# Second and fourth layer: their first tiles on unnormed, weighted latents, and the two normings' roots taken apart

## The chip, the cores and the metric

The kernel runs on one core of a Trainium2 chip. TensorE (PE) multiplies, VectorE (DVE), ScalarE (ACT) and GpSimd (POOL) work on tiles in SBUF and PSUM, and SyncE (SP) issues the DMAs. The metric is the device time of one execution in microseconds (us), the median of several runs.

## What the kernel computes

Two blocks of two layers each, on 256 latent tokens and 256 context tokens of width 1024. Every layer norms its input, multiplies it by an input matrix, mixes tokens, and then has an MLP of width 4096. Cut to what matters here:

```python
def rms_norm(x, g):
    y = x * lax.rsqrt(jnp.mean(x * x, axis=-1, keepdims=True) + EPS)
    return y * g
def modulate(h, shift, scale):
    return h * (1 + scale) + shift
# first block, layers 0 and 1 (the first and second); second block, layers 2 and 3 (the third and fourth)
a  = modulate(rms_norm(h, norm1_g[l]), sh1, sc1)      # latents
ac = modulate(rms_norm(hc, norm1_g[l]), csh1, csc1)   # context
p, u, vs, q, k, v, gl = split(a @ w_in[l])            # layers 1 and 3 need only k and v of ac
h = h + g2 * sq_relu_mlp(modulate(rms_norm(h, norm2_g[l]), sh2, sc2), w_ff1[l], w_ff2[l])
```

The root belongs to a token, gain and shift to a channel. So (gain*h*root + shift) @ W = root * ((gain*h) @ W) + shift @ W: a tile can be multiplied before the root is known, if its result is scaled by the root and shift @ W is added.

## The kernel before, in words

Everything is held with channels on the partitions: `h` is 8 chunks of 128 channels, each with 256 latent and 256 context columns. A float32 product is made of three matmuls: ACT rounds a tile to `w_h` (lines 1505 to 1513, `round_w`), DVE writes the rest to `w_l` (line 1987, in `split_w`), and inputs are split in the same way into `a_h` and `a_l`. Weights come in tiles of 256 columns (1 MB) through a ring of four slots in SBUF; SP loads a slot again when its tile has been split. Each engine follows its own list of work, written out phase by phase, and waits on semaphores.

The phases around the change are the end of one layer's second MLP product (`to_h` with source `ff`, 16 steps; its last step ends channels 4 to 7) and the entry of the next layer (`norm`, then `b1_in` in the second layer and `s_in` in the fourth). Before the change such an entry goes so:
- DVE adds the last four units to `h` (line 2474). POOL squares and adds the chunks (lines 2756 and 2758), DVE squares the last (line 2485). PE averages over channels with two matmuls (lines 1076 and 1078), for latents and context together, and ACT makes the inverse root (lines 1498 and 1499).
- In the second layer's entry a share of a modulation tile is also summed by DVE between the units (line 2020) and turned by PE (line 984). The PE then transposes a spare tile (line 933, `stay_awake`) 6 times, in the fourth layer's entry 24 times.
- For each of 8 chunks DVE multiplies by gain and root (line 2166, `scaled`), ACT adds the shift and rounds (line 1545, `rounded_norm`), and DVE writes the rest (line 2176, `rest_norm`). First come the latents' 8 chunks. The context's 8 follow: in the second layer among the next tiles (`CTX_CHUNKS`: four chunks, two, two), in the fourth all behind the third tile's split.
- PE takes the first two tiles together, chunk by chunk as they come (`first_tiles`, lines 886 to 891). The fourth layer's third tile needs latents and context (columns 0 to 511), the second layer's third to fifth need latents alone, the sixth both.
- SP loads the new layer's tables (lines 763 to 771, the bias windows at 749) once the last unit has been added to `h`, and only then the ring's next tiles.

The same trick that the change brings to the entry is there already in the MLPs' first tiles: `round_raw`, `rest_raw`, `scale_unit`, `shifted_relu`, `raw_tiles`.

## Time and profile before

| | |
|---|---|
| three runs | 2147.72 us median, 2146.95 to 2152.74 |
| profiled execution | 2148.89 us, span 2147.1 us |
| PE busy | 2097.4 us, 98% of the span |
| DVE busy | 1577.3 us, 73% |
| ACT, POOL busy | 908.8 us, 42%; 461.3 us, 21% |
| entry of the second layer | PE's last MLP matmul at 773.6, first tile at 782.0, third tile at 795.4 |
| entry of the fourth layer | last MLP matmul at 1808.7, first tile at 1814.6, third tile at 1828.4 |

The span is the time from the first to the last instruction that the profiler saw; the execution's own time holds some 1.8 us more around it. PE is busy nearly everywhere, so a change counts by what it does to the few waits of PE, and those lie where one layer hands over to the next.

### The profile page before, as it was taken

How to read it: one execution, taken by the hardware profiler on the slowest of the kernel's cores; microseconds unless marked ns; L12 is line 12 of the kernel's file. 1: busy time of each engine (PE TensorE's matmuls, PEld its weight loads, DVE VectorE, ACT ScalarE, POOL GpSimd, SP SyncE). 2: the span in 40 equal slices, each digit the busy share in tenths (PEclk: the TensorE clock that was granted, in tenths of full speed). 3: DMA queues.
4: the chain of work that ended last, by engine and by line, in shares of the span. 5: the costliest groups of instructions: out<-in, count | busy, mean ns of one | idle time of the engine just before them, and what ended most of it. 6: DMA issues, size and time to landing. Idle time of an engine off the chain costs nothing.

```text
span 2147.1 us, 31174 instructions
## 1 busy us (share of the span) xinstructions
PE 2097.4 (98%) x12421; PEld 1791.0 (83%) x12421; DVE 1577.3 (73%) x2398; ACT 908.8 (42%) x1411; POOL 461.3 (21%) x387
## 2 busy tenths in 40 slices
PE   7999999999999999999999999999999999999998
PEld 4887778888888878899999888778888888759998
DVE  6685667799778886777988777769966664687465
ACT  4313333342333342455444647754233333365454
POOL 0001210322301010212451273322222011204301
PEclk9999999999999999999999999999999999999999
DMA  9642234457675663345766442133766553415552
GB/s 302 227 139 70 67 98 138 157 166 244 239 253 178 215 184 117 117 149 195 237 228 204 138 158 89 50 118 118 235 204 207 190 167 85 99 40 158 177 194 82
DMA packets 247433, 345.36 MB, mean 161 GB/s; under 512 B 31168, under 2 KB 181608, under 8 KB 246520
## 3 DMA queue, kind: packets, MB, share of 16 engines
q1 hardware_dynamic: 245792, 339.11, 48.9%
q10 hardware_dynamic: 1496, 4.24, 0.6%
q8 instruction: 99, 1.62, 0.3%
q14 instruction: 46, 0.38, 0.0%
HBM read 342.23 MB, written 1.10 MB: 160 GB/s over the span
## 4 chain that ended last, share of the span: by engine, by line
PE 84%; DVE 7%; ACT 3%; issue 2%; POOL 2%; DMA 1%; SPq 0%; DVEq 0%; POOLq 0%; ACTq 0%
PE PS L836 24%; PE PS L838 24%; PE PS L837 24%; DVE w_l L1987 2%; PE PS L1129 1%; PE PS L1152 1%; PE PS L1138 1%; POOL h L2743 1%; DMA ring<-in_w_in 1%; PE PS L891 1%; ACT w_h L1512 1%; PE PS L1340 1%; PE PS L886 1%; PE PS L1431 1%; DVE a_l L2176 1%
## 5 line engine op out<-in xcount | busy, mean ns | idle before, releaser
L836 PE MATMUL PS<-a_h,w_h 128*128 128x512 f32 (+1 forms) x2560 | 879.9, 344 | 9.0 <-DVE a_l L2121 4.9
L838 PE MATMUL PS<-a_h,w_l 128*128 128x512 f32 (+1 forms) x2560 | 871.4, 340 | 0.0
L837 PE MATMUL PS<-a_l,w_h 128*128 128x512 f32 (+1 forms) x2560 | 871.2, 340 | 0.0
L1987 DVE TENSOR_TENSOR w_l<-ring,w_h 128x1024 fp32r<-128x1024 f32 (+1 forms) x406 | 520.2, 1322 | 260.2 <-ACT w_h L1512 259.0
L1512 ACT ACTIVATE w_h<-ring 128x1024 fp32r<-128x1024 f32 (+1 forms) x406 | 398.9, 1033 | 453.5 <-PE PS L838 445.1
L836 PEld LDWEIGHTS PS<-a_h,w_h 128*128 128x128 f32 x2560 | 486.2, 190 | 82.7 <-issue 26.9
L837 PEld LDWEIGHTS PS<-a_l,w_h 128*128 128x128 f32 x2560 | 486.4, 190 | 53.9 <-issue 1.2
L838 PEld LDWEIGHTS PS<-a_h,w_l 128*128 128x128 f32 x2560 | 486.2, 190 | 54.1
L2784 POOL TENSOR_TENSOR hid<-hid 128x256 f32<-128x256 f32 (+1 forms) x128 | 143.9, 1129 | 384.4 <-ACT hid L1494 307.4
L2052 DVE CUSTOM_DVE_ANT_0 ring<-ring,work 128x1024 f32<-128x1024 f32 x156 | 201.8, 1309 | 0.7 <-DVE mod L2052 0.7
L1494 ACT ACTIVATE hid<-PS 128x512 f32<-128x512 f32 (+1 forms) x124 | 61.6, 500 | 297.1 <-PE PS L838 297.1
L2052 DVE CUSTOM_DVE_ANT_0 bias<-ring,work 128x1024 f32<-128x1024 f32 x92 | 129.0, 1402 | 15.0 <-ACT work L1597 9.8
L2121 DVE TENSOR_TENSOR a_l<-hid,a_h 128x2048 fp32r<-128x2048 f32 (+1 forms) x60 | 108.2, 1804 | 8.7 <-ACT a_h L1537 8.7
L1494 ACT ACTIVATE big<-PS 128x256 f32<-128x256 f32 (+1 forms) x90 | 40.5, 464 | 173.2 <-PE PS L838 165.3
L836 PE MATMUL PS<-m_h,w_h 128*128 128x512 f32 (+1 forms) x320 | 109.0, 341 | 1.9 <-DVE m_l L2680 1.1
L838 PE MATMUL PS<-m_h,w_l 128*128 128x512 f32 (+1 forms) x320 | 107.5, 336 | 0.0
L837 PE MATMUL PS<-m_l,w_h 128*128 128x512 f32 (+1 forms) x320 | 107.5, 336 | 0.0
L2756 POOL TENSOR_TENSOR work<-h 128x256 f32<-128x256 f32 (+1 forms) x49 | 55.5, 1133 | 228.4 <-DVE h L2474 228.4
L836 PE MATMUL PS<-w_h,a_h 128*128 128x256 f32 x336 | 97.8, 291 | 1.7 <-DVE w_l L1987 1.7
L2813 POOL TENSOR_TENSOR bias<-windows,aux 128x256 f32<-128x256 f32 x32 | 29.4, 943 | 307.2 <-DVE mod L2084 190.8
L838 PE MATMUL PS<-w_h,a_l 128*128 128x256 f32 x336 | 95.0, 283 | 0.0
L837 PE MATMUL PS<-w_l,a_h 128*128 128x256 f32 x336 | 95.0, 283 | 0.0
(269 smaller groups left out, 2783.3 us busy)
## 6 DMA issues: line engine op xcount, KB each, us to landing
ring<-in_w_ff SPq DMA_DIRECT2D x64, 1024.0 KB, 5.5
ring<-in_ffn_w SPq DMA_DIRECT2D x64, 1024.0 KB, 5.4
ring<-in_ada_w_2T SPq DMA_DIRECT2D x44, 1024.0 KB, 5.0
ring<-in_w_in SPq DMA_DIRECT2D x42, 1024.0 KB, 5.5
ring<-in_w_modT SPq DMA_DIRECT2D x40, 1024.0 KB, 5.0
ring<-in_mlstm_w_in SPq DMA_DIRECT2D x12, 1024.0 KB, 5.8
ring<-in_w_mod SPq DMA_DIRECT2D x8, 1024.0 KB, 5.2
ring<-in_w_o SPq DMA_DIRECT2D x8, 1024.0 KB, 5.1
```

Source lines behind the costliest of these rows:

```text
L836: nc.tensor.matmul(out, stat[0], mov[0], start=start, stop=False, **kw)
L837: nc.tensor.matmul(out, stat[0], mov[1], start=False, stop=False, **kw)
L838: return nc.tensor.matmul(out, stat[1], mov[0], start=False, stop=stop, **kw)
L886: nc.tensor.matmul(outs[i][j], a[0], a[1], start=(n == 0), stop=False, **kw)
L1494: nc.scalar.activation(out, PS[0:m, bank_of[u], src_cols], func, **kw).then_inc(s_free[bank_of[u]], 1)
L1512: nc.scalar.activation(w_h[:, n % 2, c], raw[:, c], ACT.Copy).then_inc(s_wh, 1)
L1987: V.tensor_tensor(w_l[:, n % 2, c], ring[:, slot_of[split_raw[n]], c], w_h[:, n % 2, c].bitcast(F32), ALU.subtract).then_inc(s_wl, 1)
L2052: ins = V.tensor_tensor_reduce(out, w[:, j, :], silu_now[:, v, :], 1.0, 0.0, ALU.mult, ALU.add, mod[:, layer % 2, 4 * b + 2 * half + j, v: ...
L2121: V.tensor_tensor(lo, hid[:, 4 * (g % 8):4 * (g % 8) + 4, 0:cols], hi.bitcast(F32), ALU.subtract).then_inc(s_xl, 1)
L2756: nc.gpsimd.tensor_tensor(sqb[:, k % 2, c], x, x, ALU.mult).then_inc(s_pool, 1)
L2784: nc.gpsimd.tensor_tensor(x, x, x, ALU.mult).then_inc(s_ff, 1)
L2813: ins = nc.gpsimd.tensor_tensor(bias[:, a, c].rearrange("p (i c) -> p i c", i=4), shifted, aux[:, A_MASK + LAT * qt:A_MASK + LAT * qt + LA ...
```

## The change

- `RAW_ENTRY = {1: 1, 3: 2}`: one tile of layer 1 (the second) and two of layer 3 (the fourth) are multiplied from `gain*h`, which ACT rounds into `m_h` (`round_entry`) and DVE completes in `m_l` (`rest_entry`), chunk by chunk, while the layer before still ends. Two more columns carry the shift. PE puts the latents' mean after the fifth chunk of the first such tile and the context's mean behind the tile (`entry_tiles`, `mean_of`).
- The root of the latents and that of the context are two steps on ACT, each of 256 columns.
- DVE multiplies the entry tile's result by the root (`scale_entry`), ACT adds the shift (`shifted_entry`); both stand among the norming of the latents' chunks. There also stand the rounding and splitting of the weight tiles that follow.
- In the second layer the first two tiles change places (`input_part`): the branch `u` leads, since its result has channels on the partitions. The second tile is normed as before.
- `stay_awake` goes from both entries. SP loads `pool_win` of the second layer (1 MB, into memory that `m_h` now uses) later, once the entry tile is done.

```diff
+            def entry_tiles(ph, tiles):
+                n0, norm = raw_count(ph, 0), plan[plan.index(ph) - 1]
+                for i, st in enumerate(tiles):
...
+                    for k in range(KC):
...
+                        pe.wait_ge(s_rawl, n0 + k + 2)
...
+                        if i == 0 and k == 4:
+                            mean_of(norm, 4, slice(0, LAT)).then_inc(s_sqm, 1)
+                    if i == 0:
+                        mean_of(norm, 5, slice(LAT, ALL)).then_inc(s_ctxmean, 1)
...
-                        if ph["layer"] == 1 and ph["which"] == 0:
-                            mod_unit(late_step)
-                            stay_awake(6, 5)
-                        elif not ph["final"]:
+                        if not ph["final"]:
                             stay_awake(30 if ph["squares"] == "joined" else w // 128 * 2 + 16)
...
-                        first_tiles(ph["x"] - 2 * KC, (steps[0], tok), (steps[1], chans))
+                        entry_tiles(ph, steps[:1])
+                        mod_unit(late_step)
+                        first_tiles(ph["x"] - 2 * KC, (steps[1], tok))
...
+                            if k == 1:
+                                act.wait_ge(s_ctxmean, entry_nth(ph) + 1)
+                                inverse_root(rs[:, LAT:ALL], PS[:, 5, 0:CTX]).then_inc(s_ctxroot, 1)
+                                if ph["entry"] == 2:
+                                    round_w(ph["s"] + 2)
+                                shifted_entry(nx, 0)
+                                shifted_entry(nx, 1)
+                            elif k in (4, 6):
+                                round_half(ph["s"] + 1 + ph["entry"], k // 2 - 2)
...
+                        for c in {13: (0,), 14: (1,), 15: (2, 3)}.get(i, ()) if entry_of(ph) else ():
+                            rest_entry(ph, c)
...
+                            if entry_of(ph) and i == 15:
+                                for c in (range(3 + j, 4 + j) if 0 < j < 3 else (6, 7) if j else ()):
+                                    rest_entry(ph, c)
```

What moves on the engines shows in three places. The first is DVE at the end of the first layer, from the addition of the sixth channel chunk to the split of the second tile; before:

```order
L2474 SCALAR_TENSOR_TENSOR h<-PS,mod,h 128x256 [waits unit_done]
L2474 SCALAR_TENSOR_TENSOR h<-PS,mod,h 128x256
L2020 SCALAR_TENSOR_TENSOR bias<-ring,silu,bias 128x512 [waits dve_step,weights_loaded_0]
L2020 SCALAR_TENSOR_TENSOR bias<-ring,silu,bias 128x512 [waits dve_step]
L2474 SCALAR_TENSOR_TENSOR h<-PS,mod,h 128x256 [waits unit_done]
L2474 SCALAR_TENSOR_TENSOR h<-PS,mod,h 128x256
L2485 TENSOR_TENSOR work<-h 128x512 [waits bank_evacuated_3]
L2020 SCALAR_TENSOR_TENSOR bias<-ring,silu,bias 128x512 [waits dve_step,weights_loaded_0]
L2020 SCALAR_TENSOR_TENSOR bias<-ring,silu,bias 128x512 [waits dve_step]
L1987 TENSOR_TENSOR w_l<-ring,w_h 128x1024 [waits unit_done,weights_rounded] x2
```

and the same stretch with the change:

```order
L2612 SCALAR_TENSOR_TENSOR h<-PS,mod,h 128x256 [waits unit_done]
L2612 SCALAR_TENSOR_TENSOR h<-PS,mod,h 128x256
L2309 SCALAR_TENSOR_TENSOR m_l<-h,gain,m_h 128x256 [waits unnormed_rounded]
L2120 SCALAR_TENSOR_TENSOR bias<-ring,silu,bias 128x512 [waits dve_step,weights_loaded_0]
L2120 SCALAR_TENSOR_TENSOR bias<-ring,silu,bias 128x512 [waits dve_step]
L2612 SCALAR_TENSOR_TENSOR h<-PS,mod,h 128x256 [waits unit_done]
L2612 SCALAR_TENSOR_TENSOR h<-PS,mod,h 128x256
L2623 TENSOR_TENSOR work<-h 128x512 [waits bank_evacuated_3]
L2309 SCALAR_TENSOR_TENSOR m_l<-h,gain,m_h 128x256 [waits unnormed_rounded] x2
L2120 SCALAR_TENSOR_TENSOR bias<-ring,silu,bias 128x512 [waits dve_step,weights_loaded_0]
L2120 SCALAR_TENSOR_TENSOR bias<-ring,silu,bias 128x512 [waits dve_step]
L2087 TENSOR_TENSOR w_l<-ring,w_h 128x1024 [waits unit_done,weights_rounded] x2
```

The `rest_entry` instructions (L2309) stand between the additions to `h` and the shares of the modulation tile. The second place is DVE in the second layer's entry, at the end of the latents' norming. `work<-h,gain,work` and `a_l<-work,mod,a_h` are `scaled` and `rest_norm`; before, the context's first four chunks follow at once, and the split of the third tile stands behind them:

```order
L2176 SCALAR_TENSOR_TENSOR a_l<-work,mod,a_h 128x256 [waits input_rounded] x2
L2166 SCALAR_TENSOR_TENSOR work<-h,gain,work 128x256 [waits input_split] x2
L2176 SCALAR_TENSOR_TENSOR a_l<-work,mod,a_h 128x256 [waits input_rounded] x2
L2166 SCALAR_TENSOR_TENSOR work<-h,gain,work 128x256 [waits input_split] x2
L2176 SCALAR_TENSOR_TENSOR a_l<-work,mod,a_h 128x256 [waits input_rounded] x2
L1987 TENSOR_TENSOR w_l<-ring,w_h 128x1024 [waits unit_done,weights_rounded] x2
```

and with the change:

```order
L2276 SCALAR_TENSOR_TENSOR a_l<-work,mod,a_h 128x256 [waits input_rounded] x2
L2095 TENSOR_TENSOR w_l<-ring,w_h 128x1024 [waits weights_rounded] x2
L2266 SCALAR_TENSOR_TENSOR work<-h,gain,work 128x256 [waits input_split,entry_context_inverse_deviation_ready]
L2266 SCALAR_TENSOR_TENSOR work<-h,gain,work 128x256 [waits input_split]
L2276 SCALAR_TENSOR_TENSOR a_l<-work,mod,a_h 128x256 [waits input_rounded] x2
L2266 SCALAR_TENSOR_TENSOR work<-h,gain,work 128x256 [waits input_split] x2
L2276 SCALAR_TENSOR_TENSOR a_l<-work,mod,a_h 128x256 [waits input_rounded] x2
```

The third tile's split (L2095) now stands ahead of the context's chunks. The third place is DVE in the fourth layer's entry; what stands between the latents' last chunk and the context's first is, before:

```order
L2176 SCALAR_TENSOR_TENSOR a_l<-work,mod,a_h 128x256 [waits input_rounded] x2
L2637 TENSOR_SCALAR nsink<-sink 128x16 [waits tables_loaded]
L1987 TENSOR_TENSOR w_l<-ring,w_h 128x1024 [waits unit_done,weights_rounded] x2
L2166 SCALAR_TENSOR_TENSOR work<-h,gain,work 128x256 [waits input_split] x2
L2176 SCALAR_TENSOR_TENSOR a_l<-work,mod,a_h 128x256 [waits input_rounded] x2
```

and with the change:

```order
L2276 SCALAR_TENSOR_TENSOR a_l<-work,mod,a_h 128x256 [waits input_rounded] x2
L2095 TENSOR_TENSOR w_l<-ring,w_h 128x1024 [waits weights_rounded]
L2316 TENSOR_SCALAR shifted<-PS 128x2 [waits unit_done]
L2318 TENSOR_TENSOR big<-PS,work 128x256
L2316 TENSOR_SCALAR shifted<-PS 128x2 [waits unit_done]
L2318 TENSOR_TENSOR big<-PS,work 128x256
L2095 TENSOR_TENSOR w_l<-ring,w_h 128x1024 [waits weights_rounded]
L2778 TENSOR_SCALAR nsink<-sink 128x16 [waits tables_loaded]
L2266 SCALAR_TENSOR_TENSOR work<-h,gain,work 128x256 [waits input_split,entry_context_inverse_deviation_ready]
```

The split there before was the third tile's; now that one stands further ahead, among the latents' chunks, and the one here is the fourth tile's, which before came after the context's chunks.

## Rows read from the trace of the kernel before

**Rows 1.** The page, busy time of each engine

```profile
PE 2097.4 (98%) x12421; PEld 1791.0 (83%) x12421; DVE 1577.3 (73%) x2398; ACT 908.8 (42%) x1411; POOL 461.3 (21%) x387
```

**Rows 2.** Timeline, PE, second layer's entry: start, length, engine, line, operation, [idle before <-releaser]

```profile
773.60 0.39 PE L838 MATMUL PS<-a_h,w_l 128*128 128x512 f32 x1
776.74 1.12 PE L1076 MATMUL PS<-work,unit 128*128 128x512 f32 x2 [2.75 <-POOL work L2758]
...
781.98 0.35 PE L886 MATMUL PS<-w_h,a_h 128*128 128x256 f32 x1
...
795.38 0.39 PE L836 MATMUL PS<-w_h,a_h 128*128 128x256 f32 x1 [1.66 <-DVE w_l L1987]
...
815.17 0.47 PE L836 MATMUL PS<-a_h,w_h 128*128 128x512 f32 x1 [0.37 <-DVE w_l L1987]
```

**Rows 3.** Timeline, DVE, second layer's entry

```profile
767.07 2.19 DVE L2020 SCALAR_TENSOR_TENSOR bias<-ring,silu,bias 128x512 f32<-128x512 f32 x2
...
777.16 1.41 DVE L2020 SCALAR_TENSOR_TENSOR bias<-ring,silu,bias 128x512 f32<-128x512 f32 x2
...
780.75 0.87 DVE L2166 SCALAR_TENSOR_TENSOR work<-h,gain,work 128x256 f32<-128x256 f32 x2
...
788.44 0.87 DVE L2166 SCALAR_TENSOR_TENSOR work<-h,gain,work 128x256 f32<-128x256 f32 x2
...
791.35 0.88 DVE L2176 SCALAR_TENSOR_TENSOR a_l<-work,mod,a_h 128x256 fp32r<-128x256 f32 x2 [0.18 <-ACT a_h L1545]
794.10 2.36 DVE L1987 TENSOR_TENSOR w_l<-ring,w_h 128x1024 fp32r<-128x1024 f32 x2 [1.86 <-ACT w_h L1512]
...
813.83 2.36 DVE L1987 TENSOR_TENSOR w_l<-ring,w_h 128x1024 fp32r<-128x1024 f32 x2 [0.80 <-ACT w_h L1512]
```

**Rows 4.** Chain of waits, second layer's entry: start, length, what

```profile
776.51 0.28 SPq L763
...
781.16 11.82 DMA ring<-in_w_in
```

**Rows 5.** Timeline, PE, fourth layer's entry

```profile
1809.81 1.12 PE L1076 MATMUL PS<-work,unit 128*128 128x512 f32 x2 [0.72 <-POOL work L2758]
...
1828.44 0.47 PE L886 MATMUL PS<-a_h,w_h 128*128 128x512 f32 x1 [2.13 <-ACT a_h L1545]
...
1841.04 1.02 PE L1014 MATMUL PS<-big,aux 128*128 128x256 f32 x4
```

**Rows 6.** Timeline, DVE, fourth layer's entry

```profile
1813.33 0.88 DVE L2166 SCALAR_TENSOR_TENSOR work<-h,gain,work 128x256 f32<-128x256 f32 x2 [0.33 <-ACT work L1499]
...
1824.99 2.36 DVE L1987 TENSOR_TENSOR w_l<-ring,w_h 128x1024 fp32r<-128x1024 f32 x2 [3.80 <-ACT w_h L1512]
1827.27 0.88 DVE L2166 SCALAR_TENSOR_TENSOR work<-h,gain,work 128x256 f32<-128x256 f32 x2
```

**Rows 7.** Stretches: length, busy of PE, PEld, DVE, ACT, POOL, granted clock, DMA, GB/s

```profile
779.00:781.90 2.90, 2.90 (x15) 2.69 (x13) 2.66 (x5) 1.90 (x4) 0.00 (x0) 0.57 0.96 384
...
1830.00:1832.80 2.80, 2.80 (x8) 2.17 (x7) 2.44 (x7) 1.46 (x4) 0.00 (x0) 0.50 1.12 217
```

**Rows 8.** Timeline, DVE, into the fourth layer's MLP, where two tiles are unnormed already

```profile
1949.25 1.35 DVE L2194 SCALAR_TENSOR_TENSOR raw_l<-h,gain,raw_h 128x256 fp32r<-128x256 f32 x2
...
1956.14 0.88 DVE L2166 SCALAR_TENSOR_TENSOR work<-h,gain,work 128x256 f32<-128x256 f32 x2
...
1959.89 2.77 DVE L1987 TENSOR_TENSOR w_l<-ring,w_h 128x1024 fp32r<-128x1024 f32 x2
1962.58 0.83 DVE L2176 SCALAR_TENSOR_TENSOR a_l<-work,mod,a_h 128x256 fp32r<-128x256 f32 x1
...
1968.09 1.22 DVE L1995 TENSOR_TENSOR w_l<-ring,w_h 128x1024 fp32r<-128x1024 f32 x1
...
1970.02 1.21 DVE L1995 TENSOR_TENSOR w_l<-ring,w_h 128x1024 fp32r<-128x1024 f32 x1
```

**Rows 9.** Timeline, ACT, in the same place

```profile
1960.10 0.90 ACT L1570 ACTIVATE hid<-hid,shifted 128x256 f32<-128x256 f32 x2
```

More of the change, by code:

```diff
@@ L31 @@
 RAW_FIRST = (0, 1, 2, 3)
+RAW_ENTRY = {1: 1, 3: 2}
 URAW = ALL + 2
@@ L106, in phase @@
             ph["raw"] = False
+            ph["entry"] = RAW_ENTRY.get(ph["layer"], 0) if ph["which"] == 0 else 0
             ph["squares"] = {0: "first", 4: "joined"}.get(n["norm"], "layer")
@@ L597, in segs, with raw_before, raw_count, raw_units @@
             return [(0, slice(0, LAT))] + ([(1, slice(LAT, ALL))] if width == ALL else [])
-        def raw_count(ph):
-            return (KC + 1) * sum(layer in RAW_FIRST for layer in range(ph["layer"]))
-        def raw_units(ph):
-            return sum((2 if layer % 2 == 0 else 4) for layer in RAW_FIRST if layer < ph["layer"])
+        def raw_before(ph, which):
+            return [(layer, w) for layer in range(4) for w in range(2)
+                    if (layer in RAW_FIRST if w else layer in RAW_ENTRY) and (layer, w) < (ph["layer"], which)]
+        def raw_count(ph, which=1):
+            return (KC + 1) * len(raw_before(ph, which))
+        def raw_units(ph, which=1):
+            return sum((2 if layer % 2 == 0 else 4) if w else 2 * RAW_ENTRY[layer] for layer, w in raw_before(ph, which))
+        def entry_of(ph):
+            norms = [p for p in plan if p["kind"] == "norm" and p["which"] == 0 and p["layer"] == ph["layer"] + 1]
+            return norms[0] if norms and norms[0]["entry"] and ph["src"] == "ff" else None
+        def entry_nth(ph):
+            return sorted(RAW_ENTRY).index(ph["layer"])
+        def entry_out(ph, i):
+            return uT[:, i, 0:LAT] if ph["block"] == 0 else sq_[:, i, :]
         def raw_cols(s):
@@ L798, in _ @@
                         load_tables(ph)
+                    if kind == "b1_in" and ph["layer"] == 1 and st is ph["steps"][2]:
+                        sp.wait_ge(s_unit, ph["steps"][0]["u"] + 2)
+                        load_win()
                     if ph.get("name") in ("w_o", "m_out") and st is ph["steps"][1]:
@@ L1066, in _ @@
                     w = ph["width"]
-                    if ph["squares"] == "first" or ph["raw"]:
+                    if ph["squares"] == "first" or ph["raw"] or ph["entry"]:
                         pass
@@ L1562, in round_raw, with round_entry, shifted_entry @@
                 ins.then_inc(s_rawh, 1)
+            def round_entry(ph, c):
+                nx = entry_of(ph)
+                now = nx["layer"] % 2
+                if c == 0:
+                    act.wait_ge(s_mcol, mod_unit_of[nx["layer"], 3] + 1)
+                    act.wait_ge(s_xl, ph["x"] + 12)
+                wait_unit(act, ph["steps"][7 if c < 4 else 15]["u"] + c % 4)
+                if c == 0:
+                    shift = mod[:, now, 0:KC, 0:1].broadcast_to([P, KC, 2])
+                    nc.scalar.activation(m_h[:, :, LAT:LAT + 2], shift, ACT.Copy).then_inc(s_rawh, 1)
+                nc.scalar.activation(m_h[:, c, 0:LAT], h[:, c, 0:LAT], ACT.Copy, scale=gain[:, now, 0, c, 0:1]
+                                     ).then_inc(s_rawh, 1)
+            def shifted_entry(ph, i):
+                act.wait_ge(s_scaledu, raw_units(ph, 0) + i + 1)
+                x = entry_out(ph, i)
+                nc.scalar.activation(x, x, ACT.Identity, bias=shifted[:, i, 0:1], scale=1.0 if ph["block"] == 0 else QSCALE
+                                     ).then_inc(s_free[bank_of[ph["steps"][i // 2]["u"] + i % 2]], 1)
             def shifted_relu(ph, i):
@@ L1690, in _ @@
                         round_hidden(ph, i + 1)
+                        if entry_of(ph) and i >= 12:
+                            round_entry(ph, i - 12)
+                    for c in range(4, KC) if entry_of(ph) else ():
+                        round_entry(ph, c)
                 elif kind == "to_h":
@@ L2197, in rest_raw, with rest_entry, scale_entry @@
                 ins.then_inc(s_rawl, 1)
+            def rest_entry(ph, c):
+                nx = entry_of(ph)
+                n0, now = raw_count(nx, 0), nx["layer"] % 2
+                if c == 0:
+                    dve.wait_ge(s_rawh, n0 + 1)
+                    shift = mod[:, now, 0:KC, 0:1].broadcast_to([P, KC, 2])
+                    V.tensor_tensor(m_l[:, :, LAT:LAT + 2], shift, m_h[:, :, LAT:LAT + 2].bitcast(F32), ALU.subtract
+                                    ).then_inc(s_rawl, 1)
+                dve.wait_ge(s_rawh, n0 + c + 2)
+                V.scalar_tensor_tensor(out=m_l[:, c, 0:LAT], in0=h[:, c, 0:LAT], scalar=gain[:, now, 0, c, 0:1],
+                                       in1=m_h[:, c, 0:LAT].bitcast(F32), op0=ALU.mult, op1=ALU.subtract).then_inc(s_rawl, 1)
+            def scale_entry(ph, i):
+                u = ph["steps"][i // 2]["u"] + i % 2
+                dve.wait_ge(s_unit, u + 1)
+                V.tensor_scalar(shifted[:, i, :], PS[:, bank_of[u], LAT:LAT + 2], 1.0 if ph["block"] == 0 else QSCALE, None,
+                                ALU.mult)
+                V.tensor_tensor(entry_out(ph, i), PS[:, bank_of[u], 0:LAT], rs[:, 0:LAT], ALU.mult).then_inc(s_scaledu, 1)
             def scale_unit(ph, i):
```

65 lines of the change are left out of this document (54 added, 11 removed).

## The prediction

> **What bounds the kernel now.** I read the page first: PE is busy 98% of the span [rows 1], so the time is PE's, and only its waits can be won or lost. The timeline of PE shows where they are. In the second layer's entry PE ends the MLP at 773.6 + 0.4 = 774.0 and starts the first tile at 781.98: 8.0 us, in which it waits 2.75 for POOL's sum and then does averages, turning and spare transposes; before the third tile it waits 1.66 for a split weight tile, before the sixth 0.37 [rows 2]. In the fourth layer's entry the third tile waits 2.13 [rows 5].
>
> Then I asked who ends those waits late: DVE. In the second layer's entry the third tile's split starts at 794.10, after 1.86 us of waiting for ACT, and the sixth tile's at 813.83, for which PE is already waiting [rows 2, 3]. ACT itself stood still for a DMA: the chain of waits holds 11.82 us from 781.16 to 793.0 in which that tile was loaded, behind tables that SP issues from 776.51 on [rows 4]. In the fourth layer's entry the third tile waits for the context's first chunk, whose norming starts at 1827.27 behind a split that began at 1824.99 after 3.80 us of waiting [rows 6]. So DVE, in program order, sets when PE goes on in both places, and has 1.9 and 3.8 us of slack.
>
> **The change part by part.** The times of one execution are its own: the sum is made against 2148.89 us.
>
> *The lead waits go, and that alone gives nothing.* PE can start the entry tiles at 774.0 and 1809.1. Two tiles take 11.74 us (781.98 to 793.72, where the wait of 1.66 begins), so a matmul of 256 columns takes 11.74/96 = 0.122 us and a tile 5.9. In the second layer one tile leaves the road behind the root, in the fourth two. But PE's next tiles hang on DVE's list, so what counts is when DVE gets there.
>
> *Second layer, DVE up to the root.* DVE has no gap here: between the units it sums shares of the modulation tile (767.07 to 777.16 + 1.41), then it splits the second tile, and at 780.75 scales the first chunk [rows 3]. Eight `rest_entry` come in; the first two lie in steps with idle time, six on this chain. Alone, two instructions of this form take 0.87 [rows 3], beside POOL 1.35 [rows 8]. Four alone and two beside POOL: 1.74 + 1.35 = 3.1 us. The root is not later than that: before, its means started at 776.74 [rows 2], 4.0 us ahead of the first scaled chunk, and the last square comes 2.2 later (0.87 + 1.35 ahead of it). First scaled chunk: 780.75 + 3.1 = 783.85. If POOL hid none or all of them: 2.6 to 4.1.
>
> POOL's effect on DVE is visible: the pair of sums takes 2.19 beside POOL and 1.41 alone [rows 3]. The Trainium skill (SBUF — State Buffer, section "SBUF: two separate sides") says that a DVE instruction with two SBUF inputs and a GpSimd instruction exclude each other wholly, rather than share. By that rule the two `rest_entry` beside POOL might cost as much extra as the pairs of sums show, 0.8 each instead of 0.24, and the result would be 1.1 us later; the trace's 1.35 for a pair is a partial slowing, so it does not bear the rule out in full for this form.
>
> *Second layer, the latents' norming.* Before, 780.75 to 788.44: 7.7 us. The fourth layer's MLP has the same list with two unnormed tiles in it [rows 8]. There it is 3.75 us from the first scaled chunk to the end of the two scaled units (1956.14 to 1959.89), then come ACT's two shifts, 0.90 [rows 9], and its next chunk, some 0.15, and from DVE's third `rest_norm` to the split of the weights 5.5 us (1962.58 to 1968.09). Together 10.3, ending at 794.15. Two half splits, 2.4, end at 796.5, where before the split ended at 796.46. The difference is the context: before, its first four chunks were done by 792.23 (788.44 to 791.35 + 0.88), now they stand behind the split. That is 3.8 us more in front of the fourth tile's split and of all that follows up to the sixth tile, where DVE had 0.80 us of slack and PE none.
>
> *Second layer, the load.* SP issues the tables once the last unit is added, which four of the six `rest_entry` push back by the same 2.2. Without `pool_win` the queue holds 1 MB less ahead of the third tile, at 384 GB/s [rows 7] 2.7 us. The tile lands at 793.0 + 2.2 - 2.7 = 792.5. ACT wants it after the fifth chunk, about 783.85 + 4.8 + 1.8 = 790.4, and waits 2.1 us with three chunks of the latents queued behind it, so DVE waits too. Bounds: 0 (landed in time) and 2.8 (`pool_win` gone gives half of that). I take 2.1. Second layer: 3.8 + 2.1 = 5.9, between 3.3 (0.5 less norming and no wait) and 7.6 (1.0 more of POOL, 0.7 more of the load). PE's fourth tile would start near 806 instead of 801, after a wait of 3 us.
>
> *Fourth layer.* Before, the means started at 1809.81, the first scaled chunk at 1813.33. Now five chunks go first: 30 x 0.122 = 3.7 from 1809.1, so means at 1812.8, 3.0 later; half the columns in averages and root give back some 1.2 (estimate: half of the 1.12 shown for each average), and the wait of 0.72 and the spare transposes no longer matter. First scaled chunk 1814.4 to 1815.1; I take 1814.4, since the averages need no further wait. From there the MLP's list is the same word for word to the end of the last half split: 1956.14 to 1970.02 + 1.21 = 15.1 us [rows 8]. The context's first chunk at 1829.5 instead of 1827.27: 2.2 later. PE, done with both tiles near 1822, waits until 1830.7 and starts the third tile 2.2 later than before. Bounds: -1.5 (if the root is early and the split finds its tile ready) to +4. The clock was low after the wait of before already (0.50 from 1830.0 to 1832.8 [rows 7]) and will be again, so nothing is added for it here.
>
> *The rest.* The reversed order of two tiles, ACT's eight roundings, two more matmuls for the means and the later `pool_win` cost nothing: ACT is busy 42% [rows 1], and `pool_win` is needed only at the end of the fifth tile. If that cover went, each would cost under 1 us.
>
> Sum: 5.9 + 2.2 = 8.1, so 2157.0 for the profiled execution. The median of the runs lies 1.2 below that execution; on that footing 2155.8 us.
>
> **Rivals.**
>
> *The head start holds (faster).* PE gets both entries' work early, so if DVE kept up, it would save the lead waits: in the fourth layer the third tile could start at 1822 instead of 1828.44, 6.4 us, in the second up to 5. The point that decides is the fourth layer's DVE list from the first scaled chunk to the context: under 1827.27 - 1814.4 = 12.9 us PE gains. For it: 3.8 us of waiting leave that list [rows 6]. Against: the same list measured 15.1 [rows 8]. With half of the saving the time is near 2142, with all of it 2137.
>
> *Half of the loss only.* The third tile lands in time (the tables need not queue as I reckon), and the fourth layer's root is early: 3.3 to 3.8 in the second, 0 in the fourth, so some 2151. For it: the bounds above; DVE's waits for ACT are short and may shrink.
>
> *PE's clock takes more.* PE now waits 3 us before the second layer's fourth tile and 9 us in the fourth layer, where before it waited 1.66 and 2.13. After 2.13 us of waiting the granted clock fell to 0.50, the lower level, for most of 3 us, and after 2.75 it stood at 0.57 [rows 7]. A low stretch costs half its length, 1.4 us; a new one in the second layer and a longer one in the fourth make 2.8 on top: 2158.6. The Trainium skill (TensorE: Matmul & The Clock Gate, section "HAM oscillation — how this bites in real kernels") names this: gaps between bursts make the next burst start cold. The rows agree that it happens; that a longer gap costs more no row here shows.
>
> **How the numbers follow.** This kernel's measurement tells changes from about 0.3%, 6.4 us, that is below 2141.3 or above 2154.2. Forecast, both entries later by about 8 in all: 0.54. Clock on top: 0.09. Half of the loss: 0.28. Head start holds: 0.09, of which 0.06 go beyond 0.3%. The forecast's own range reaches from 2152 to 2160; of its 0.54, some 0.08 lie under 2154.2. Slower 0.54 - 0.08 + 0.09 = 0.55, faster 0.06, same 0.08 + 0.28 + 0.03 = 0.39. For 8 in 10 the range leaves out the gain and takes in half of the loss and the clock: 2146 to 2161.
>
> **What would show it.** Right: in the second layer's entry PE starts within 0.5 us of the MLP's end, DVE's first scaled chunk is near 784 where the MLP ends at 774.0, ACT waits for the third tile's DMA among the latents' chunks, the fourth tile's split starts about 5 us later, and the sixth tile about 6. In the fourth layer DVE's list takes 15 us and PE waits 8 to 9 us before the third tile. Wrong: a third tile in the fourth layer that starts under 19 us after the MLP's end, or a sixth tile in the second within 41 us of it.

## The result and the profile after

The change made the kernel slower. Five runs of it have a median of 2158.50 us (2156.26 to 2159.45), five of the kernel before 2150.05 (2146.95 to 2152.74); the ratio is 1.0038, with a 95% interval of 1.0025 to 1.0051. The same kernel run again beside others gave 2158.69 against 2148.60, a ratio of 1.0050 (1.0037 to 1.0062). So the loss is 8 to 10 us, under half a percent; in both the interval leaves out 1. Later runs of the kernel before on one chip fall into two groups, nine of 2146.57 to 2149.13 us and eleven of 2151.04 to 2153.76, the slower at the lower mean granted clock (0.994 to 0.996 against 0.996 to 0.998), so a ratio below need not be that of the two medians beside it. The profiled execution after took 2159.45 us, its span is 2157.7 us, 10.6 more than before. The page's busy times hardly moved against [rows 1]; the time went into waits.

```profile
PE 2096.8 (97%) x12399; PEld 1791.6 (83%) x12399; DVE 1590.1 (74%) x2428; ACT 916.4 (42%) x1433; POOL 461.2 (21%) x387
```

The timeline of PE in the second layer's entry answers to [rows 2] (start, length, engine, line, operation, idle before and who ended it):

```profile
773.49 0.39 PE L871 MATMUL PS<-a_h,w_l 128*128 128x512 f32 x1
773.72 0.28 PE L869 MATMUL PS<-m_h,w_h 128*128 128x258 f32 x1
...
795.26 0.58 PE L919 MATMUL PS<-w_h,a_h 128*128 128x256 f32 x1 [2.93 <-ACT a_h L1604]
...
807.60 0.39 PE L869 MATMUL PS<-a_h,w_h 128*128 128x256 f32 x1 [2.72 <-DVE w_l L2087]
...
822.66 0.50 PE L869 MATMUL PS<-a_h,w_h 128*128 128x512 f32 x1
```

PE goes straight from the MLP into the entry tile; the 8.0 us of [rows 2] without a tile are gone. In their place come shorter waits, the longest of them 2.93 among the latents' chunks and 2.72 before the fourth tile, and the sixth tile starts at 822.66 instead of 815.17. DVE's timeline, against [rows 3], ends with the first copy behind the sixth tile:

```profile
771.30 3.22 DVE L2120 SCALAR_TENSOR_TENSOR bias<-ring,silu,bias 128x512 f32<-128x512 f32 x2
...
775.62 3.20 DVE L2120 SCALAR_TENSOR_TENSOR bias<-ring,silu,bias 128x512 f32<-128x512 f32 x2
...
784.64 0.88 DVE L2266 SCALAR_TENSOR_TENSOR work<-h,gain,work 128x256 f32<-128x256 f32 x2
...
795.25 0.48 DVE L2276 SCALAR_TENSOR_TENSOR a_l<-work,mod,a_h 128x256 fp32r<-128x256 f32 x1 [2.95 <-ACT a_h L1604]
...
797.39 2.35 DVE L2095 TENSOR_TENSOR w_l<-ring,w_h 128x1024 fp32r<-128x1024 f32 x2
...
806.32 2.36 DVE L2087 TENSOR_TENSOR w_l<-ring,w_h 128x1024 fp32r<-128x1024 f32 x2 [1.00 <-ACT w_h L1571]
...
820.84 2.36 DVE L2087 TENSOR_TENSOR w_l<-ring,w_h 128x1024 fp32r<-128x1024 f32 x2 [0.80 <-ACT w_h L1571]
...
828.48 0.69 DVE L2074 COPY big<-PS 128x512 f32<-128x512 f32 x1 [2.34 <-PE PS L871]
```

The splits of the third, fourth and sixth tile start at 797.39, 806.32 and 820.84; before, the sixth's started at 813.83 and the fourth's here:

```profile
799.32 2.36 DVE L1987 TENSOR_TENSOR w_l<-ring,w_h 128x1024 fp32r<-128x1024 f32 x2 [1.01 <-ACT w_h L1512]
```

From the fourth to the sixth split DVE takes 14.5 us in both kernels, so what DVE loses it loses ahead of the fourth: that split starts 806.32 - 773.49 = 32.8 us after the last matmul of the MLP, before 799.32 - 773.60 = 25.7, 7.1 later. ACT's timeline names the DMA, as [rows 4] did:

```profile
793.76 1.06 ACT L1580 ACTIVATE w_h<-ring 128x1024 fp32r<-128x1024 f32 x1 [2.75 <-DMA ring<-in_w_in]
```

and SP's shows the first of the tables that go ahead of that load, at 779.77 instead of 776.51:

```profile
779.77 0.28 SPq L792 DMA_DIRECT2D aux<-in_sgub  x1
```

In the fourth layer's entry, PE against [rows 5] and DVE against [rows 6] (all there is 8.06 us later than before, 1817.19 against 1809.13 at the last addition to `h`):

```profile
1838.41 0.76 PE L919 MATMUL PS<-a_h,w_h 128*128 128x512 f32 x1 [8.04 <-ACT a_h L1604]
```

```profile
1817.19 0.88 DVE L2612 SCALAR_TENSOR_TENSOR h<-PS,mod,h 128x256 f32<-128x256 f32 x2 [0.37 <-PE PS L871]
...
1822.63 0.87 DVE L2266 SCALAR_TENSOR_TENSOR work<-h,gain,work 128x256 f32<-128x256 f32 x2
...
1834.10 1.22 DVE L2095 TENSOR_TENSOR w_l<-ring,w_h 128x1024 fp32r<-128x1024 f32 x1
...
1837.24 0.88 DVE L2266 SCALAR_TENSOR_TENSOR work<-h,gain,work 128x256 f32<-128x256 f32 x2
...
1851.54 1.29 DVE L2074 COPY big<-PS 128x512 f32<-128x512 f32 x2 [6.77 <-PE PS L924]
```

PE stands 8.04 us before the third tile, because the context's first chunk is scaled at 1837.24, 14.6 us after the latents' first. The clock, against [rows 7] (length, busy of PE, PEld, DVE, ACT, POOL, granted clock, DMA, GB/s), is at the lower level (0.50) behind the waits of 2.72 and 8.04:

```profile
808.90:812.20 3.30, 3.30 (x18) 3.30 (x17) 3.08 (x8) 3.09 (x6) 0.18 (x1) 0.50 0.63 203
...
1838.40:1843.00 4.60, 4.59 (x11) 3.63 (x12) 4.23 (x11) 2.09 (x5) 0.00 (x0) 0.50 1.11 216
```

Two distances sum this up, and every run below is read by them. A is from the last matmul of the first layer's MLP to the first copy behind the second layer's sixth tile: 828.48 - 773.49 = 54.99 us, before 820.89 - 773.60 = 47.29, so 7.7 lost. B is from the last addition to `h` in the third layer to the first copy behind the fourth layer's third tile: 1851.54 - 1817.19 = 34.35, before 1841.01 - 1809.13 = 31.88, so 2.5 lost. Together 10.2 of the 10.6 that the spans differ by. The ends of A and B before, and the start of B, are these:

```profile
820.89 0.69 DVE L1974 COPY big<-PS 128x512 f32<-128x512 f32 x1 [1.76 <-PE PS L838]
...
1809.13 0.88 DVE L2474 SCALAR_TENSOR_TENSOR h<-PS,mod,h 128x256 f32<-128x256 f32 x2 [1.85 <-PE PS L838]
...
1841.01 1.29 DVE L1974 COPY big<-PS 128x512 f32<-128x512 f32 x2 [2.86 <-PE PS L891]
```

### The profile page after: what moved, and what is told of

It reads as the page before. It is cut to its first block, busy times and chain, and to the rows that moved or that the text cites. A ratio compares the mean times of both kernels' runs of the same rounds, so it can differ in the third digit from the quotient of the medians.

```text
span 2157.7 us, 31188 instructions
## 1 busy us (share of the span) xinstructions
PE 2096.8 (97%) x12399; PEld 1791.6 (83%) x12399; DVE 1590.1 (74%) x2428; ACT 916.4 (42%) x1433; POOL 461.2 (21%) x387
## 4 chain that ended last, share of the span: by engine, by line
PE 85%; DVE 7%; ACT 3%; issue 2%; DMA 2%; POOL 0%; SPq 0%; DVEq 0%; ACTq 0%; POOLq 0%
PE PS L869 25%; PE PS L871 25%; PE PS L870 25%; DVE w_l L2087 1%; PE PS L1188 1%; PE PS L1211 1%; PE PS L1197 1%; DMA ring<-in_w_in 1%; DVE a_l L2276 1%; PE PS L1399 1%; PE PS L1490 1%; DVE work L2266 1%; PE PS L924 1%; PE PS L919 1%; PE PS L920 1%
## 5 line engine op out<-in xcount | busy, mean ns | idle before, releaser
L869 PE MATMUL PS<-m_h,w_h 128*128 128x512 f32 (+2 forms) x368 | 123.1, 335 | 1.9 <-DVE m_l L2821 1.1
L871 PE MATMUL PS<-m_h,w_l 128*128 128x512 f32 (+2 forms) x368 | 121.1, 329 | 0.0
L870 PE MATMUL PS<-m_l,w_h 128*128 128x512 f32 (+2 forms) x368 | 121.1, 329 | 0.0
```

The costliest lines, as they stand in the source:

```text
L869: nc.tensor.matmul(out, stat[0], mov[0], start=start, stop=False, **kw)
L870: nc.tensor.matmul(out, stat[0], mov[1], start=False, stop=False, **kw)
L871: return nc.tensor.matmul(out, stat[1], mov[0], start=False, stop=stop, **kw)
```

## The experiments

| kernel | median, us | before beside it | ratio (95%) | A | B |
|---|---|---|---|---|---|
| before (first profile) | | | | 47.29 | 31.88 |
| the change again | 2158.69 | 2148.60 | 1.0050 (1.0037 to 1.0062) | 54.91 | 34.50 |
| fourth layer only | 2151.99 | 2147.41 | 1.0021 (1.0012 to 1.0030) | 47.62 | 35.01 |
| second layer only | 2155.13 | 2147.41 | 1.0036 (1.0022 to 1.0050) | 55.02 | 30.28 |
| early load | 2155.64 | 2147.41 | 1.0040 (1.0028 to 1.0053) | 52.26 | 35.12 |
| context first, second layer | 2157.97 | 2147.41 | 1.0053 (1.0040 to 1.0066) | 53.91 | 34.57 |
| awake | 2156.34 | 2148.60 | 1.0041 (1.0027 to 1.0055) | 54.86 | 32.46 |
| late shares moved, early load | 2155.17 | 2148.60 | 1.0033 (1.0020 to 1.0045) | 45.42 | 35.03 |
| context first, fourth layer | 2155.27 | 2148.60 | 1.0033 (1.0021 to 1.0046) | 55.52 | 31.54 |
| combined | 2144.17 | 2151.09 | 0.9977 (0.9967 to 0.9986) | 45.43 | 30.02 |
| combined, context two by two | 2142.56 | 2151.09 | 0.9971 (0.9959 to 0.9983) | 44.70 | 29.54 |
| before, relieved | 2145.12 | 2151.09 | 0.9977 (0.9969 to 0.9986) | 43.56 | 31.84 |
| second layer undone | 2142.47 | 2148.64 | 0.9970 (0.9961 to 0.9979) | 43.30 | 29.25 |

Kernels with the same number for before ran on one chip with it; A and B are from each one's profile, a single execution. In the edits `...` marks what is left out.

**Each part alone.** The first kernel keeps the fourth layer's part, the second the second layer's; the other layer's code is that of before.

```diff
-RAW_ENTRY = {1: 1, 3: 2}
+RAW_ENTRY = {3: 2}
...
+RAW_ENTRY = {1: 1}
...
```

> Only the fourth layer's part of the change; the second layer's entry is as in the kernel before. Theory (DVE's list sets both entries): the second layer's sixth tile starts as before, 41.2 us after the MLP's end, and only the fourth layer's loss is left, 1.9 us at its third tile and some 0.6 of low clock behind it: 2150.05 + 2.5 = 2152.5 us. Rival (the losses are not the entries' own, the second layer's shift is given back later): about 2158. Rival (the head start in the fourth layer is worth something and only the second layer spoils it): under 2149.

> Only the second layer's part of the change; the fourth layer's entry is as before. Theory: the sixth tile of the second layer starts some 49 us after the MLP's end instead of 41.2, nothing gives it back, and the time is 2150.05 + 8 = 2158 us, 5.5 above the kernel with only the fourth layer's part. Rival (half of the loss only, 3.5 us): 2153.5.

Both lose, as expected: 4.6 us with the fourth layer's part, 7.7 with the second's, by the medians. A and B say that each entry carries its own loss: A is 47.62 in the first kernel and 55.02 in the second, before 47.29. The rival that the head start is worth something in the fourth layer falls. One thing was not expected: in the second kernel, whose fourth layer is coded as before, B is 30.28, 1.6 below before. PE waits 2.12 us there, as before the change (2.13), and the clock stays up (PE's row, then the stretch):

```profile
1836.68 0.47 PE L919 MATMUL PS<-a_h,w_h 128*128 128x512 f32 x1 [2.12 <-ACT a_h L1605]
```

```profile
1836.00:1842.00 6.00, 5.32 (x23) 4.43 (x24) 5.42 (x13) 3.12 (x7) 0.00 (x0) 1.00 1.14 217
```

**The load.** SP sends the third tile's load ahead of the tables.

```diff
-                    send(sent_at[split_raw[ph["s"] + 1]] + 1)
+                    send(sent_at[split_raw[ph["s"] + (2 if ph["layer"] == 1 else 1)]] + 1)
```

> The change, with the second layer's third tile loaded ahead of the tables instead of behind them; nothing else moves. Theory (ACT stands at that load with three chunks of the latents queued behind it, and DVE with it): ACT's wait of 2.75 us goes, DVE's third split starts near 794.4 instead of 797.39, the fourth near 803.4 instead of 806.32, the sixth near 817.9 instead of 820.84. PE still waits 2.5 to 3 us before the fourth tile and falls to the low clock there, so the sixth tile starts at 819.5 to 820 instead of 822.9: 2155.6 us, 2.9 less than the change. Rival (PE's clock is what costs, the load is hidden anyway): 2158.5, no gain.

DVE's splits of the third, fourth and sixth tile in that kernel:

```profile
794.50 2.35 DVE L2095 TENSOR_TENSOR w_l<-ring,w_h 128x1024 fp32r<-128x1024 f32 x2
...
803.42 2.36 DVE L2087 TENSOR_TENSOR w_l<-ring,w_h 128x1024 fp32r<-128x1024 f32 x2 [1.00 <-ACT w_h L1571]
...
817.94 2.36 DVE L2087 TENSOR_TENSOR w_l<-ring,w_h 128x1024 fp32r<-128x1024 f32 x2 [0.80 <-ACT w_h L1571]
```

Each is within 0.1 us of what was expected, and A falls by 2.7. The load is a cost of its own. The medians of the change again and of this kernel differ by 3.1 us, but their chips differ; the two intervals overlap, so it is the trace that shows it. That the median meets the expected 2155.6 is luck: the sum had started from the change at 2158.5, beside which the kernel before took 2150.05, and on this chip that one took 2147.41.

**The order of DVE's list in the second layer.** The third tile is rounded and split behind the context's first four chunks again.

```diff
-                            elif k in (4, 6):
+                            elif k in (4, 6) and ph["entry"] == 2:
                                 round_half(ph["s"] + 1 + ph["entry"], k // 2 - 2)
...
-                            elif k == KC - 1:
+                            elif k == KC - 1 and ph["entry"] == 2:
                                 split_half(ph["s"] + 1 + ph["entry"], 0)
```

> The change, with the second layer's third tile rounded and split behind the context's first four chunks again, as before the change. Prediction's step (the context's chunks behind the split cost 3.8 in front of the fourth tile's split): fourth split 3.8 earlier, 802.5, and 2154.7 us. Theory as the trace after suggests (DVE's list is as long in either order, only its waits differ: 2.95 for the load and 1.0 for the fourth tile's rounding now, 1.0 before each of two splits then): fourth split near 804.3, 2.0 earlier, no wait of PE in front of the fourth tile and so no low clock there, sixth tile 2.0 + 0.9 earlier: 2155.6 us. Rival (the late root alone sets it): 2158.5.

DVE did what the theory said (the fourth split, first line, is 2.7 us earlier by its distance from the MLP's end; the prediction's step would have made it 3.8), but A fell by 1.1 only, and the time shows nothing of it. The split is late for the third tile instead, and PE waits once, for longer; behind it the clock is low for 5.7 us, half of which is lost by the granted clock of 0.50:

```profile
803.86 2.36 DVE L2087 TENSOR_TENSOR w_l<-ring,w_h 128x1024 fp32r<-128x1024 f32 x2 [1.00 <-ACT w_h L1571]
```

```profile
799.93 0.58 PE L869 MATMUL PS<-w_h,a_h 128*128 128x256 f32 x1 [4.85 <-DVE w_l L2087]
```

```profile
799.90:805.60 5.70, 5.67 (x26) 5.67 (x27) 4.52 (x7) 3.34 (x6) 0.00 (x0) 0.50 1.10 350
```

So my expectation of 2155.6 failed: a wait of PE moved forward and made whole cost what the shorter wait behind it saved.

**The clock.** Spare transposes stand in the waits.

```diff
                     entry_tiles(ph, steps[:2])
+                    stay_awake(64)
...
+                        if i == 3 and ph["l"]:
+                            stay_awake(20, 5)
```

> The change, with spare transposes of PE in its two long waits: 64 in the fourth layer's, which lasted 8.04 us (24 took 2.78, so 7.4 us), and 20 in front of the second layer's fourth tile, where it waited 2.72. Theory (the low clock after a wait is a cost of its own on top of DVE's list): the fourth layer's third tile starts when it did, but at the full clock, 2.3 us less; the second layer's sixth tile is 0.7 to 0.9 earlier: 3.1 us less than the change. Rival (the clock comes back in time anyway, or the transposes only move the low stretch): no difference.

In the fourth layer the transposes hold the clock at the upper level, and B falls by 2.0 against the change again:

```profile
1827.88 7.15 PE L993 MATMUL PS<-ident 128*128 128x128 f32 x64
1836.36 0.47 PE L919 MATMUL PS<-a_h,w_h 128*128 128x512 f32 x1 [1.33 <-ACT a_h L1607]
```

```profile
1836.30:1843.00 6.70, 6.64 (x29) 5.55 (x30) 5.86 (x14) 3.04 (x7) 0.00 (x0) 1.00 1.12 223
```

Of the 3.1 us expected these 2.0 came, and the medians fell by 2.4. For the second layer the run tells nothing: A is the same to 0.1, but in the profile of the change again the clock had not fallen behind the fourth tile either. What the clock costs there stays open.

**The late modulation tile.** Its four shares and two sums leave DVE's list ahead of the sixth tile; the early load is in.

```diff
...
                                 copy_unit(u + j, kT[:, 2 * (i - 5) + j, :], slice(0, 512))
+                                if ph["l"] == 1 and i == 5:
+                                    last = last if j else [None, None]
+                                    mod_tile(late_step["parts"][-1][0], late_step, last, range(2 * j, 2 * j + 2))
...
-                            if st["late"]:
-                                key = st["parts"][-1][0]
-                                last = [None, None] if j == 0 else last
-                                mod_tile(key, st, last, range(j, j + 1))
```

> The change with the early load of the second layer's third tile, and with DVE's four shares of the late modulation tile (10.0 us in the trace after, 2.19 + 3.22 + 3.20 + 1.41) and its two sums taken out from between the first layer's last units and put behind the second layer's sixth tile; the ring slot of that tile is given back later. Theory (DVE's list from the last units to the sixth tile's split is what counts): first scaled chunk near 780 instead of 784.6, sixth tile's split near 812 instead of 820.84, the first copy behind the sixth tile 7 to 9 us earlier than with the change, so 2150 to 2152 us if the change itself is at 2158.5. Rival (the root and POOL's squares, not DVE's list, set the first chunk): the first chunk stays above 783 and the gain is the load's 2.9 and the sums' 1.4 alone. Rival (the shares cost the same where they stand now, or the later slot holds the seventh tile's load): the first copy is earlier but the next tiles wait, and the time is 2155 or more.

DVE, and PE at the seventh tile:

```profile
779.59 0.88 DVE L2270 SCALAR_TENSOR_TENSOR work<-h,gain,work 128x256 f32<-128x256 f32 x2 [0.29 <-ACT work L1562]
...
811.36 2.36 DVE L2091 TENSOR_TENSOR w_l<-ring,w_h 128x1024 fp32r<-128x1024 f32 x2 [0.80 <-ACT w_h L1575]
...
825.22 2.73 DVE L2124 SCALAR_TENSOR_TENSOR bias<-ring,silu,bias 128x512 f32<-128x512 f32 x4
```

```profile
829.01 0.55 PE L872 MATMUL PS<-a_h,w_h 128*128 128x512 f32 x1 [2.71 <-DVE m_l L2372]
```

Up to the sixth tile the theory holds to 0.7 us (779.6 for 780, 811.4 for 812), and A falls by 9.6, below before. Then the last rival comes true: the shares at 825.22 stand ahead of the small units on DVE, PE waits 2.71 for one of these, and with the low clock behind it the third such copy comes 5.3 us earlier than with the change by its distance from the MLP's end, not 9.6. The time is 2155.17, not 2150 to 2152.

**The order of DVE's list in the fourth layer.**

```diff
...
-                                split_half(ph["s"] + 1 + ph["entry"], 0)
-                                if ph["entry"] == 2:
-                                    scale_entry(nx, 2)
-                                    scale_entry(nx, 3)
...
+                            context_norm(plan[plan.index(ph) - 1], range(4))
+                            scale_entry(ph, 2)
+                            scale_entry(ph, 3)
+                            context_norm(plan[plan.index(ph) - 1], range(4, KC))
```

> The change, with the fourth layer's fourth tile rounded and split behind the context's chunks again, and the second entry tile scaled between the context's chunks instead of ahead of them. Theory (DVE's list from the first scaled chunk, 14.6 us, sets the third tile): the list is shorter by two half splits and two scaled units, 2.4 + 1.0 = 3 to 3.4 us, the third tile of the fourth layer starts that much earlier, and the time is 3 us less than the change's. Rival (the second tile's split or the root sets it): the list is as long as before and nothing is gained. Rival (the fourth tile's split is then late): PE waits in front of the fourth tile what it gained.

```profile
1832.99 0.77 PE L919 MATMUL PS<-a_h,w_h 128*128 128x512 f32 x1 [5.13 <-ACT a_h L1604]
```

The third tile starts 18.3 us after the last addition to `h`, with the change 1838.41 - 1817.19 = 21.2: 2.9 less for 3 expected. The median fell by 3.4, and PE does not wait for the fourth tile. DVE's list sets that tile.

**All repairs together.** The early load, the moved shares and sums, the fourth layer's context ahead of its fourth tile, and spare transposes in both waits. The shares now go two behind the first unit of the sixth tile and two behind that of the seventh; the last line of the diff is the second kernel's alone.

```diff
...
+                                if ph["l"] == 1 and j == 0:
+                                    last = last if i == 6 else [None, None]
+                                    mod_tile(late_step["parts"][-1][0], late_step, last, range(2 * i - 10, 2 * i - 8))
...
-        CTX_CHUNKS = {0: range(0, 4), 1: range(4, 6), 2: range(6, 8)}
+        CTX_CHUNKS = {0: range(0, 2), 1: range(2, 4), 2: range(4, 6), 3: range(6, 8)}
```

> The change with four repairs together: the early load, the late modulation's shares behind the first units of the sixth and seventh tile (two each; the run with all four behind the sixth left PE waiting 2.71 us for the seventh) and its sums behind them, the fourth layer's context ahead of its fourth tile, and spare transposes in the two waits (18 and 40). Theory: in the second layer the first copy behind the sixth tile at 819 (before 820.89) and nothing given back, in the fourth layer 29.2 us from the last addition to h to the first copy behind the third tile (before 31.88, after 34.35): 1.8 + 2.7 = 4.5 us less than the kernel before, a ratio of 0.998. Rival (the shares cost the same wherever they stand): no less than before, a ratio of 1.000 to 1.001.

> The combined kernel, with the context's chunks of the second layer two by two among four tiles instead of four, two and two, and 10 transposes in place of 18 there. Theory (PE's 2.92 us of waiting for the fourth tile's split come from four context chunks ahead of it): that split is 1.86 earlier, the wait 1.0, and the sixth tile 0.8 earlier, where its own split is then the later one: 0.8 us less than the combined kernel. Rival: no difference.

Both beat the kernel before, 0.9977 and 0.9971, and nothing of A is given back. Taking the context two by two lowered A by 0.7; in the times the two can't be told apart.

**What the change itself is worth.** The kernel before with the early load and the moved shares and sums (and 14 transposes where the turning and 6 stood), and the combined kernel with the second layer's entry as before the change.

```diff
...
-                        entry_tiles(ph, steps[:1])
-                        first_tiles(ph["x"] - 2 * KC, (steps[1], tok))
+                        first_tiles(ph["x"] - 2 * KC, (steps[0], tok), (steps[1], dict(stays=True, n=cols)))
```

> The kernel before, without the change, with the early load and the late modulation's shares and sums moved as in the combined kernel (14 transposes where there were the turning and 6). Theory (DVE's list, not the lead wait, is what the second layer's entry costs): the first scaled chunk some 2 us earlier (778.7), the third split near 790.7, the sixth tile 3.7 us earlier than before: 2145 to 2146 us where before is 2148.6, so as much as the combined kernel gains in that entry, and the change itself is worth nothing there. Rival (PE's head start is what such a relief sets free): the gain stays under 1.5 us.

> The combined kernel with the context two by two, but the second layer's entry multiplied as before the change (two normed tiles, no unnormed one); the fourth layer keeps the unnormed tiles and its two repairs. Theory (even relieved, the second layer's entry is set by DVE's list, and the unnormed tile only makes it longer): from the last matmul of the first layer's MLP to the first copy behind the sixth tile 42.8 us, where the kernel before has 47.3, the relieved kernel before 43.6 and the combined kernels 45.4 and 44.7; the fourth layer 29.6 from the last addition to h to the first copy, as in the combined kernels: 1.9 us less than the combined kernel with the context two by two, a ratio of 0.996 to 0.997 to the kernel before. Rival (the unnormed tile is worth something once DVE's list is short): 44.7 or more, and a time no less than that kernel's.

The last matmul of the MLP, and the first copy behind the sixth tile, in the relieved kernel before:

```profile
772.03 0.39 PE L841 MATMUL PS<-a_h,w_l 128*128 128x512 f32 x1
```

```profile
815.59 0.69 DVE L1978 COPY big<-PS 128x512 f32<-128x512 f32 x1 [3.01 <-PE PS L841]
```

A is 43.56 without the change and 45.43 with it, where the entry differs only by the change's part in it and by the number of transposes; with the context two by two, 43.30 without and 44.70 with it. So even with a short list the change's part makes the second layer's entry 1.4 to 1.9 us longer. In the times that does not show (0.9970 and 0.9971). In the fourth layer the repaired tiles give a B of 29.25 to 30.02, before it is 31.88 with a low clock and 30.28 without: the tiles with their repairs are worth 0.3 to 1.0 (against the one execution with 30.28), the rest is the clock that the transposes hold. Nearly the whole gain of the combined kernels is the moved shares, the earlier load and the clock.

## Why the prediction was right, step by step

The direction, the mechanism and the size were right: 8.1 us forecast, 8.4 and 10.1 measured by the medians. By the trace A and B lost 10.2, so that the first medians lie so near to 8.1 is in part luck. The second layer took more than its range allowed: 5.9 forecast, between 3.3 and 7.6, and 7.7 measured; its fourth split came 7.1 later and its sixth tile 7.6, where about 5 and 6 were named as signs. By its terms:

- *The lead waits give nothing by themselves.* Right. PE started the entry tile 0.2 us after the MLP's last matmul, and gained nothing in either entry.
- *DVE up to the root, +3.1.* Mis-sized: the first scaled chunk came 784.64 - 773.49 = 11.15 us after that matmul, before 7.15, so 4.0 later. The six instructions took 2.6 by the starts behind them, 0.5 less than reckoned. What was not reckoned is that the two middle pairs of sums, which the change leaves as they were, take 3.22 and 3.20 beside POOL, 0.8 more each than before (the last section shows how):

```profile
769.97 2.44 DVE L2020 SCALAR_TENSOR_TENSOR bias<-ring,silu,bias 128x512 f32<-128x512 f32 x2
...
773.12 2.44 DVE L2020 SCALAR_TENSOR_TENSOR bias<-ring,silu,bias 128x512 f32<-128x512 f32 x2
```

- *The latents' norming, 10.3 instead of 7.7, and the context behind the split.* Right in size: without the load's wait the list takes 794.50 - 784.53 = 10.0 (early load). With the step above, the fourth split is 4.4 us later there than before, for 3.8. The cause that was named holds only in part. The 3.8 were put down to the context's chunks behind the split. With four of them ahead of it again, the fourth split came 803.86 - 773.69 = 30.2 us after the MLP's last matmul; in the new order without the load's wait it was 803.42 - 773.33 = 30.1. So DVE's list is as long in either order, and the order decides only whether the load's wait is covered.
- *The load, +2.1.* Mechanism right, size 2.7: the tile came at 793.76 instead of 792.5, since the last addition to `h`, and SP's tables with it, were 3.3 later rather than 2.2. The upper bound of 2.8 doesn't follow from what is said of it: with half of the 2.7 for `pool_win` the wait would be 2.1 + 1.35 = 3.5.
- *Fourth layer, +2.2.* Right in size: first scaled chunk 1.2 later by its distance for 1.1, a list of 14.6 for 15.1, a wait of 8.04 for 8 to 9, the third tile 1.9 later. The forecast had the root set the first chunk. The root was ready at 1822.57 (ACT's last step, 1822.15 + 0.42), but DVE's own list, which the forecast left out here, ended in the same moment: the square, 0.69 before, took 1.55 beside POOL's last sum, then came two `rest_entry` and the split, and the chunk at 1822.63 followed without a wait:

```profile
1818.10 1.55 DVE L2623 TENSOR_TENSOR work<-h 128x512 f32<-128x512 f32 x1
```

- *Nothing for the clock.* Here the forecast was short, and the rival that PE's clock takes more has its share: 0.6 in the fourth layer (from the third tile to the first copy behind it 1851.54 - 1838.41 = 13.1 us instead of 1841.01 - 1828.44 = 12.6), and 0.5 in the second, in this execution: there the sixth tile started 1.82 after its split did, before 815.17 - 813.83 = 1.34. In the profile of the change again, where the clock had not fallen behind the fourth tile, it was 820.86 - 819.52 = 1.34 again, though its A is no smaller, since its splits came 0.5 later.

Together 4.4 + 2.7 + 0.5 + 1.9 + 0.6 = 10.1, where A and B lost 10.2. The other rivals fell: the head start did not hold (each part alone loses), and half of the loss was too little, since the load was late, not in time, and the fourth layer lost too.

## What to carry to other kernels

A head start for PE is worth something only if the engine that feeds it has room: add up that engine's list from the last unit to the next tiles first, since on a list with hardly a gap, as here, what is added comes back as waits of PE. What freed time here was to take work out of that list that nobody needed yet, and its new place has to be read as carefully as the old one: the same shares gave back 4 us in one place and nothing one tile further on. And a load that stands behind tables on a queue was late with them, here by 2.7 us.

## What the hardware showed that was not expected

- The clock does not follow the length of a wait alone. In the fourth layer's entry coded as before, PE waited 2.13 us in one run and 2.12 in another; behind the first the granted clock was 0.50 for most of 3 us [rows 7], behind the second 1.00. Before the second layer's fourth tile it waited 2.92 us both with the early load and with the late shares moved, and the clock behind it was 0.50 in the one and 1.00 in the other:

```profile
804.70 0.39 PE L869 MATMUL PS<-a_h,w_h 128*128 128x256 f32 x1 [2.92 <-DVE w_l L2087]
```

```profile
806.00:808.00 2.00, 2.00 (x12) 2.00 (x11) 1.82 (x5) 1.79 (x5) 0.00 (x0) 0.50 0.44 91
```

```profile
799.78 0.39 PE L872 MATMUL PS<-a_h,w_h 128*128 128x256 f32 x1 [2.92 <-DVE w_l L2091]
```

```profile
801.00:803.00 2.00, 2.00 (x19) 2.00 (x19) 1.54 (x4) 1.71 (x5) 0.00 (x0) 1.00 0.42 82
```

  The Trainium skill (TensorE: Matmul & The Clock Gate, section "HAM oscillation — how this bites in real kernels") has the next burst start cold after a gap that is too long. The waits of 2.72, 4.85 and 8.04 us agree; these two pairs show the same wait go either way.
- A pair of sums on DVE takes 1.41 us alone [rows 3], and beside POOL's squares and sums 2.44 before and 3.2 after. The single instructions show how; before, with the first sum of the pair at 769.97:

```profile
769.97 0.99 DVE L2020 SCALAR_TENSOR_TENSOR bias<-ring,silu,bias 128x512 f32<-128x512 f32 x1
```

```profile
770.38 1.49 POOL L2756 TENSOR_TENSOR work<-h 128x512 f32<-128x512 f32 x1
```

  and after, with a `rest_entry` ahead of the pair:

```profile
770.65 0.72 DVE L2309 SCALAR_TENSOR_TENSOR m_l<-h,gain,m_h 128x256 fp32r<-128x256 f32 x1
771.30 1.52 DVE L2120 SCALAR_TENSOR_TENSOR bias<-ring,silu,bias 128x512 f32<-128x512 f32 x1
```

```profile
771.05 1.22 POOL L2897 TENSOR_TENSOR work<-h 128x512 f32<-128x512 f32 x1
...
772.35 1.61 POOL L2899 TENSOR_TENSOR work<-work 128x512 f32<-128x512 f32 x1
```

  The two engines end in turn. Before, DVE's first sum ends at 770.96, POOL's square 0.91 later, DVE's second sum 0.54 after that (769.97 + 2.44). After, `rest_entry` ends at 771.37, POOL's square 0.90 later, DVE's first sum 0.55 after that, POOL's sum 1.14 after that, and DVE's second sum 0.56 after that (771.30 + 3.22). So the same turn takes as long in both kernels. But `rest_entry` now takes the turn ahead of the square, so the pair meets the square and POOL's sum, and before it met the square and only the end of a sum (from 768.79, 1.62 long). The Trainium skill (SBUF — State Buffer, section "SBUF: two separate sides") says that the engine that starts first holds the port, and the other is shut out whole. The turns agree with it. The pair of 1.35 [rows 8], which the prediction took for a partial slowing, agrees as well: its first instruction took 0.95 and ended 0.3 after POOL's, its second 0.47, as alone. No run took `rest_entry` alone out of the list, so this is read from the order of the ends.
